# Seven levels of a recurrence's small products issued in three bursts between large products instead of four

## The reference, cut to what matters

```python
G = cumsum(log(f))                                 # per chunk of 64 tokens
A = einsum('bhtc,bhsc,bhtsc->bhts', q, k, exp(G_t - G_s))      # s <= t
o = einsum('bhts,bhsv->bhtv', A, i) + einsum('bhtc,bhcv->bhtv', q * exp(G), S)
```

## Time and profile before

| | us |
|---|---|
| median of three runs | 942.53 (942.43 to 942.7) |
| profiled execution, its own time | 943.0 |
| its span | 941.2 |
| TensorE busy in the span | 934.0 |
| VectorE, ScalarE, GpSimd busy | 698.0, 529.9, 86.0 |
| TensorE's granted clock, mean share | 0.998 |

### The profile page before, as it was taken

One profiled execution on the slowest core, in us unless ns is written; L12 is line 12 of the kernel. 1 busy time (PEld: TensorE's weight loads), 2 busy tenths in 40 slices (PEclk: granted clock), 3 DMA queues, 4 the chain that ended last, 5 costly groups with the idle time before them and its releaser, 6 DMA issues.

```text
span 941.2 us, 13594 instructions
## 1 busy us (share of the span) xinstructions
PE 934.0 (99%) x5414; PEld 800.1 (85%) x5414; DVE 698.0 (74%) x1005; ACT 529.9 (56%) x680; POOL 86.0 (9%) x150
## 2 busy tenths in 40 slices
PE   9999999999999999999999999999999999999997
PEld 9888888888888888888888888888887888888886
DVE  6998568778768778788876757578888677576675
ACT  6876866654446555555655445356755465353544
POOL 1300228082100000000000000000003000000000
PEclk9999999999999999999999999999999999999999
DMA  9855355344564554556364654653534445646451
GB/s 357 322 193 172 143 204 200 134 140 173 179 229 179 196 200 162 206 179 221 138 240 159 209 193 179 224 179 136 184 133 173 161 147 211 221 161 219 158 179 45
DMA packets 26110, 175.08 MB, mean 186 GB/s; under 512 B 3256, under 2 KB 3520, under 8 KB 6080
## 3 DMA queue, kind: packets, MB, share of 16 engines
q1 hardware_dynamic: 25168, 170.15, 49.9%
q10 hardware_dynamic: 880, 4.07, 1.2%
HBM read 173.15 MB, written 1.06 MB: 185 GB/s over the span
## 4 chain that ended last, share of the span: by engine, by line
PE 99%; DVE 0%; ACT 0%; issue 0%; POOL 0%; ACTq 0%; POOLq 0%
PE ps L425 45%; PE ps L432 30%; PE ps L436 16%; PE ps L555 1%; PE ps L653 1%; PE ps L789 1%; PE ps L805 1%; PE ps L840 1%; PE ps L711 1%; PE ps L644 0%; PE ps L773 0%; PE ps L854 0%; PE ps L820 0%; PE ps L738 0%; PE ps L889 0%; PE ps L737 0%
## 5 line engine op out<-in xcount | busy, mean ns | idle before, releaser
L1650 DVE TENSOR_TENSOR Wl<-raw,Wh 128x2048 fp32r<-128x2048 f32 x151 | 346.0, 2295 | 32.4 <-ACT Wh L1119 31.7
L1119 ACT ACTIVATE Wh<-raw 128x2048 fp32r<-128x2048 f32 x154 | 294.5, 1913 | 34.0 <-PE ps L425 30.8
L432 PE MATMUL ps<-hT,Wh 128*128 128x512 f32 x1248 | 298.4, 391 | 0.0
L432 PEld LDWEIGHTS ps<-hT,Wh 128*128 128x128 f32 x1248 | 231.6, 188 | 47.4 <-issue 1.0
L425 PE MATMUL ps<-Wh,hT 128*128 128x512 f32 (+1 forms) x640 | 198.6, 385 | 0.0
L436 PEld LDWEIGHTS ps<-hT,Wl 128*128 128x128 f32 x1248 | 159.4, 191 | 5.0
L436 PE MATMUL ps<-hT,Wl 128*128 128x256 f32 x1248 | 162.7, 283 | 0.0
L1476 ACT ACTIVATE Am<-ps 128x512 f32<-128x512 f32 x66 | 39.2, 594 | 177.1 <-PE ps L436 173.6
L425 PEld LDWEIGHTS ps<-Wh,hT 128*128 128x128 f32 x640 | 118.3, 188 | 23.7 <-issue 1.5
L1739 DVE TENSOR_TENSOR PT<-ps,Am 128x256 f32<-128x256 f32 x132 | 49.7, 419 | 105.8 <-ACT Am L1476 105.8
L425 PE MATMUL ps<-Wh,yTh 128*128 128x512 f32 (+1 forms) x314 | 122.8, 391 | 0.0
(11 more groups left out here) (273 smaller groups left out, 755.6 us busy)
## 6 DMA issues: line engine op xcount, KB each, us to landing
raw<-in_units SPq DMA_DIRECT2D x154, 1024.0 KB, 4.8
FP<-in_bias ACTq DMA_DIRECT2D x1, 2048.0 KB, 7.5
FP<-in_first SPq DMA_DIRECT2D x2, 768.0 KB, 8.4
FP<-in_first SPq DMA_DIRECT2D x3, 384.0 KB, 5.8
raw<-in_units SPq DMA_DIRECT2D x2, 512.0 KB, 10.3
X<-in_x SPq DMA_DIRECT2D x1, 1024.0 KB, 17.0
Hn<-in_mem SPq DMA_DIRECT2D x1, 1024.0 KB, 9.0
XT<-in_mem_turned SPq DMA_DIRECT2D x1, 1024.0 KB, 11.6
```

What stands on the lines that cost most here:

```text
L432: pe.matmul(o, lh(k), hT_both(k), start=first and k == ks[0], stop=False)
L1119: act.activation(wh[j % NS][:, 0:n], raw[j % NR][:, 0:n], ACT.Copy).then_inc(w_hi, 1)
L1650: dve.tensor_tensor(wl[j % NS][:, 0:n], raw[j % NR][:, 0:n], wh[j % NS][:, 0:n].bitcast(F32), ALU.subtract).then_inc(w_lo, 1)
```

## The change

TensorE issues the levels behind u = 1, 4 and 7: own and level 0; levels 1, 2, 3; levels 4, 5, 6. VectorE copies levels 1 to 3 out at u = 5 and levels 4 to 6 at u = 8. ScalarE's four copies of Near into Am move from u = 7, ahead of four sigmoids, to u = 8, between the exponential of E1 and `gate_out(9)`. No instruction is added or removed.

```diff
@@ TensorE
             def levels_after(u):
-                if u in (1, 3, 5, 7):
-                    if u == 1:
-                        own_products()
-                    for n in (u - 2, u - 1):
-                        if n >= 0:
-                            level_products(n)
+                if u == 1:
+                    own_products()
+                    level_products(0)
+                elif u in (4, 7):
+                    for n in range(u - 3, u):
+                        level_products(n)
@@ ScalarE
                 elif u == 7:
                     gate_out(6)
                     gate_out(7)
-                    act.wait_ge(*free(("lv", 4)))
-                    for x in range(0, 128, 32):
-                        act.activation(heads(Am[x:x + 32, :], 8)[:, :, x:x + 32], heads(Near[x:x + 32, :], 8),
-                                       ACT.Copy).then_inc(near_placed, 1)
                     for j in range(4):
                         gate_sigmoid(j)
                 elif u == 8:
                     gate_out(8)
                     act.wait_ge(ch_sub, 4)
                     act.activation(E1, E1, ACT.Exp).then_inc(ch_exp, 1)
+                    act.wait_ge(*free(("lv", 4)))
+                    for x in range(0, 128, 32):
+                        act.activation(heads(Am[x:x + 32, :], 8)[:, :, x:x + 32], heads(Near[x:x + 32, :], 8),
+                                       ACT.Copy).then_inc(near_placed, 1)
                     gate_out(9)
@@ VectorE
-                elif u in (4, 6, 8):
-                    level_out(u - 3)
-                    level_out(u - 2)
+                elif u in (5, 8):
+                    for n in range(u - 4, u - 1):
+                        level_out(n)
```

## The result

The changed kernel took 946.45 us (median of six runs, 945.68 to 947.48) against 942.68 for the kernel before in the same sessions: ratio 1.0039, 95% interval 1.0029 to 1.0049. It is slower by 3.8 us where 0.3 less was forecast. Its profiled execution took 945.92 us with a span of 944.1, 2.9 more than before.

A forecast was written before the change was run, and what follows sets the result against it. TensorE's own stream was taken to bound the kernel, busy 934.0 of 943.0 us. One switch saved, all else at nothing: 942.53 - 0.3 = 942.2 us, range 941.7 to 943.1.

The forecast's parts named there:

- The saving: TensorE's bursts of small matmuls: one entry into and exit from the narrow form fewer, -0.3 us; chance 0.78.
- The costs put at nothing: New waits of TensorE and the moved copies on VectorE and ScalarE: all covered by slack, 0 us.
- ScalarE's moved copies: Four Near copies ahead of gate_out(9): 0.7 us left before TensorE takes gate 5's bank; cost nothing, at most +0.4 us.
- VectorE's copies: Level copies moved to u = 5 and u = 8: the following split ends some 0.45 us later, still covered; cost nothing.
- level 3's operands: Inputs of level 3 in the long burst: the last ends at 75.86, 3.7 us before the burst; no wait.
- The bank wait: Ahead of gate 5's second part TensorE waits up to 0.4 us for ScalarE's copies: 942.3 to 942.8; chance 0.06.
- The rival "Slower": Inside the burst of 384 instructions TensorE stops for an instruction packet, 2 to 4.8 us: 944.5 to 947; chance 0.03.

The follow-up runs named there:

- number 8: Against the kernel before, levels 1 and 2 at u = 3 and levels 3 to 6 together at u = 7, repeated with more rounds: 942.28 us, ratio 0.9995.
- number 1: The changed kernel with 168 instructions that only wait, seven at each of 24 steps, ahead of the long burst: 946.64 us, ratio 1.0042.
- number 2: Against the kernel before, levels 1 and 2 at u = 3 and levels 3 to 6 together at u = 7, unpadded: 942.44 us, ratio 0.9998.
- number 7: The changed kernel with level 3 taken out of the long burst and put behind gate 2's second half: 942.81 us, ratio 1.0000.
- number 4: The kernel before with 64 instructions that only wait, four at each of 16 steps of gate 1: 943.29 us, ratio 1.0005.
- number 5: The changed kernel with 112 instructions that only wait, two at each of 56 steps ahead of the long burst: 942.49 us, ratio 0.9996.
- number 9: The kernel with levels 3 to 6 together plus 160 instructions that only wait, two at each of 80 steps: 947.61 us, ratio 1.0044.
- number 3: The kernel with levels 3 to 6 together plus 168 instructions that only wait, seven at each of 24 steps: 953.37 us, ratio 1.0106.

## Why the prediction was wrong

**The saving** was right in mechanism and size: 0.3 us for one entry into and exit from the narrow form, 0.28 in number 8. It was the whole of the sum, and it is in the changed kernel too; its cross products are 2.93 later = 0.22 at the start + 2.95 from the 183rd small matmul to the next - 0.3, within 0.1.

**The costs put at nothing** were right: ScalarE's moved copies left gate 5's bank free 0.65 us before TensorE took it, where 0.7 was foreseen (the four took 1.72 us beside VectorE's products, as before, and a wait held TensorE's sequencer for 0.1 us in number 1), VectorE's copies delayed nobody (numbers 2, 7), and level 3's operands were ready. The bank wait did not come.

**The rival "Slower"** is what happened, with its place (inside the burst of 384 instructions), its sign and its price: 944.5 to 947 against 946.45. Its 256 instructions a packet are what the trace counts (255.9, at the head of the experiments). The step that failed is the instruction fetch, put at nothing in the sum and given a chance of 0.03; the runs showed a stop of 2.8 to 3.3 us at instruction 1473, inside the burst. I argued that 256 instructions lay ready and the fetch is early, since a packet followed the first burst and none moved in it, and stopped there. I had not looked far enough back: in the kernel before, a packet started at 58.81, three us ahead of that burst. Counted back from the packet that ended the stop at 1473, it is the one for the block at 961, which TensorE entered as the burst ended. The burst was fed because a border happened to stand at its start, and not because fetches are always early. TensorE ran dry at 1473 and 1985 whatever stood there (five profiles), so the packets' contents are fixed, and the question was not whether 256 instructions lay ready but which ones: a block ends at a fixed instruction (1473 and 1985 by the stops; 1217 and 1729 follow, 256 from them), and the request for a block seems to go out near the border 256 instructions ahead of it, when the sequencer passes it (numbers 4 and 5: the packet 1.1 us behind). In the four profiles with a stop of 2.8 us or more TensorE went on 4.2 to 5.0 us after it had passed that border (80.36 to 84.58 in the changed kernel), where a burst uses up the block between in 1.2 us. In the kernel before, a burst uses up 256 instructions in 1.2 us and the hundred behind it last 11 us, so by this account time is left wherever the border falls (number 4 tried one other place). With 384 the answer depends on where the border falls. The trace of before could not have told me where the borders are, but it showed one packet to every 256 instructions or so and one packet in flight at a time; a burst that is sure to use up most of a block, with a fetch bounded between 2 and 4.8 us, meets a border in the wrong place about as often as not. With 384 instructions in the burst a whole block of 256 lies inside it for half of the possible places of the border, so the chance belonged near a half, and the range had to reach 947. That the packet may also stand behind a weight load (number 4) was not in the rival either.

**The clock** was missing altogether: in the slow profile of the changed kernel it fell inside the gap and cost 2.4 us, which with the longer gap makes 948.1 out of some 945.

## What to carry to other kernels

TensorE's instructions were a stream that had to be delivered too (43 packets, and 0.7 to 3.5 us of standing still where one came late). Before small matmuls are gathered into a longer burst, count the burst's instructions (weight loads and matmuls each) against the 256 of a packet, and ask how long the rest of the stream lasts while the next packet comes, and whether a large load is in its way. If a burst has to be longer, its place relative to the packets' borders was worth 3 to 6.6 us here (942.4 against 945.5 to 949.0), and any edit ahead of it moves it. An "issue" gap in the middle of a loop without waits may be such a fetch: adding a few harmless instructions ahead, two to a step, told it here (numbers 5 and 9). Among the kernels tried the one of numbers 2 and 8 (942.44 and 942.28) is the lowest, but what it gains over the kernel before is less than the measurement can tell and it is one shift away from 947.6.

## What the runs showed of the hardware that I had not expected

- Where TensorE ran dry it was at the same instruction whatever stood there: 1473 in three profiles of two kernels (the changed one twice, and number 1), 1985 in two kernels (numbers 3, 9).
- From the start of the packet to the next matmul it took 2.5 us in the changed kernel (82.11 to 84.58), and 2.3 to 2.9 in the other four profiles with a stop; the packet itself took 0.9 to 1.0 us in four of the five.
- The gap was 2.8 and 3.3 us in two profiles of one kernel, 3.5 in number 9. In the first of these the DMA engines were 0.89 busy with weight loads in the 2 us before, and the instruction packet started where the load ended; that it queued behind the load is argued (number 4), not tried.
- Inside such a gap the granted clock fell to 0.50 in three of four profiles that had one of 2.8 us or more (3.0, 3.3 and 3.5 us), read 0.50 for 6.8 us and cost 2.4 to 2.7 us; it stayed at 1.00 in the other (2.8 us).
- Seven instructions that only wait, at each step of three 0.227 us matmuls, cost TensorE time (numbers 1, 3: from the first burst to the long one 3.4 and 3.9 us for 24 steps); two at each step cost at most 0.2 (number 5: 52.48 us from the first burst to the cross products, where kernels with three bursts and no padding need 52.3).
